# Far values of dilated attention: transposed products from scaled probabilities, added to the near values by identity products in PSUM

## What is computed

```python
for gi, (window, dilation) in enumerate(((128, 1), (512, 4), (2048, 16))):
    o, lse = dilated_window_group(q[:, :, gi], k_sh[:, :, gi], v_sh[:, :, gi], window, dilation)
    outs.append(o)
    lses.append(lse)
alpha = jax.nn.softmax(jnp.stack(lses, axis=0), axis=0)
o = jnp.sum(alpha[..., None] * jnp.stack(outs, axis=0), axis=0)
return o.reshape(bsz, seq, ATTN_OUT_WIDTH).astype(xn.dtype) @ w_o
```

## Time and profile before

| | |
|---|---|
| median of three runs | 1446.95 us (1443.18 to 1450.6) |
| the profiled execution's own time | 1444.98 us |
| its span, first to last instruction | 1443.3 us |
| TensorE's mean granted clock | 0.966 of full |
| busy: TensorE, VectorE, ScalarE, GpSimd | 92%, 72%, 60%, 25% of the span |
| the stretch that the change touches | about 1018 to 1100 us of the span |

### The profile page before, as it was taken

How to read it: one execution, slowest core, us unless ns; L and a number is a source line. 1 busy time by engine, 2 the same in 40 slices (tenths; PEclk the granted TensorE clock), 3 DMA queues, 4 the chain that set the end, 5 groups by cost and what they waited for, 6 DMA issues and landing times. The chain is left out here.

```text
span 1443.3 us, 28422 instructions
## 1 busy us (share of the span) xinstructions
PE 1332.6 (92%) x10965; PEld 1053.9 (73%) x10965; DVE 1034.2 (72%) x1381; ACT 860.8 (60%) x1316; POOL 366.8 (25%) x413
## 2 busy tenths in 40 slices
PE   6899997898899899999996999999998999999994
PEld 3577676777754788888884787878786788888873
DVE  6556845567653799999997436666445799899997
ACT  7735644465422588888883444445544588888882
POOL 2022445466700122233311100011110133233310
PEclk9999999999999999999998999999979999999998
DMA  6322300411571699999994432112131699999994
GB/s 195 117 88 88 117 15 3 108 33 40 151 287 69 224 376 386 385 382 387 385 362 160 142 89 79 59 59 88 60 117 73 239 392 386 388 385 376 385 345 182
DMA packets 159668, 295.90 MB, mean 205 GB/s; under 512 B 16989, under 2 KB 32477, under 8 KB 159568
## 3 DMA queue, kind: packets, MB, share of 16 engines
q1 hardware_dynamic: 150416, 278.21, 53.3%
q0 software_dynamic: 8928, 16.22, 3.0%
q10 hardware_dynamic: 224, 0.07, 0.0%
HBM read 280.35 MB, written 30.41 MB: 215 GB/s over the span
## 5 line engine op out<-in xcount | busy, mean ns | idle before, releaser
L1717 DVE TENSOR_TENSOR moe_wlo<-kept_raw,moe_whi 128x2048 fp32r<-128x2048 f32 x162 | 370.2, 2288 | 42.4 <-ACT moe_whi L1713 37.8
L1713 ACT ACTIVATE moe_whi<-kept_raw 128x2048 fp32r<-128x2048 f32 x192 | 365.3, 1919 | 38.7 <-DMA kept_raw<-in_moe_w_down_dram 16.5
L1724 PE MATMUL all_bank<-moe_whi,moe_xhi 128*128 128x512 f32 x512 | 203.8, 398 | 1.1 <-DVE moe_xlo L1773 1.1
L1726 PE MATMUL all_bank<-moe_whi,moe_xlo 128*128 128x512 f32 x512 | 199.6, 390 | 0.0
L1725 PE MATMUL all_bank<-moe_wlo,moe_xhi 128*128 128x512 f32 x512 | 199.6, 390 | 0.0
L1724 PEld LDWEIGHTS all_bank<-moe_whi,moe_xhi 128*128 128x128 f32 x512 | 96.1, 188 | 23.0 <-DVE moe_xlo L1773 1.5
L1726 PEld LDWEIGHTS all_bank<-moe_whi,moe_xlo 128*128 128x128 f32 x512 | 96.1, 188 | 20.5
L1725 PEld LDWEIGHTS all_bank<-moe_wlo,moe_xhi 128*128 128x128 f32 x512 | 96.2, 188 | 18.8
L1724 PE MATMUL all_bank<-moe_whi,moe_hhi 128*128 128x512 f32 x256 | 100.3, 392 | 3.0 <-issue 2.6
L2381 DVE SCALAR_TENSOR_TENSOR attn_wlo<-attn_xhat,all_par,attn_whi 128x512 fp32r<-128x512 f32 x64 | 43.8, 747 | 78.4 <-ACT attn_whi L2364 78.4
L1726 PE MATMUL all_bank<-moe_whi,moe_hlo 128*128 128x512 f32 x256 | 99.7, 389 | 0.0
(11 more groups left out here) (458 smaller groups left out, 2916.7 us busy)
## 6 DMA issues: line engine op xcount, KB each, us to landing
kept_raw<-in_moe_w_gate_dram SPq DMA_DIRECT2D x64, 1024.0 KB, 11.1
kept_raw<-in_moe_w_up_dram SPq DMA_DIRECT2D x64, 1024.0 KB, 12.3
kept_raw<-in_moe_w_down_dram SPq DMA_DIRECT2D x64, 1024.0 KB, 11.3
attn_xhat<-in_w_kv_dram SPq DMA_DIRECT2D x10, 1024.0 KB, 5.1
attn_xhat<-in_attn_w_q_dram SPq DMA_DIRECT2D x6, 1024.0 KB, 5.0
all_h<-in_rwkv_w_k_dram SPq DMA_DIRECT2D x4, 1024.0 KB, 9.0
all_h<-in_rwkv_w_v_dram SPq DMA_DIRECT2D x4, 1024.0 KB, 5.0
all_h<-in_rwkv_w_r_dram SPq DMA_DIRECT2D x4, 1024.0 KB, 5.0
```

Of the source, the lines that this page charges most:

```text
L1713: nc.scalar.activation(whi[slot % SPLITS][:, :], raw[slot % 6][:, :], ACT.Copy).then_inc(m["hi_ok"], 1)
L1717: nc.vector.tensor_tensor(wlo[slot % SPLITS][:, :], raw[slot % 6][:, :], whi[slot % SPLITS][:, :].bitcast(fp32), ALU.subtract).then_inc(m[ ...
L1724: nc.tensor.matmul(bank[b][:, :], hi[:, k0 + k, :], wh[:, k, :], start=begin and k == 0, stop=False)
L1726: ins = nc.tensor.matmul(bank[b][:, :], lo[:, k0 + k, :], wh[:, k, :], start=False, stop=end and k == 3)
```

## The change

Far values are now made with the values as weights (128x64) and the transposed probabilities moving (128 columns), so the result comes out transposed, head e of a pair on PSUM partitions 64e to 64e + 63. The accumulated near and middle values are added in the same bank by a product with the identity (a true product, no transpose). For this the probabilities must hold the factor 1/sum before they are transposed: VectorE's new `share(u)` multiplies them in place by the reciprocals (128x512), and the transposes of the far units wait for `shared` in place of `p_ok`. `far_output` and its two VectorE instructions per pair are gone, and so are `far_values` and `turn`; `far_and_turn(b)` stands for both, for b = 0 to 2 ahead of the last unit's transposes, for b = 3 in the place of `turn(3)`. ScalarE copies the last transposed probabilities, and splits the second half of `w_o`, later in its order.

```diff
--- before.py
+++ after.py
@@ -2314,8 +2314,8 @@
             s.sem, ["squared", "rms", "rstd_ok", "xhat_ok", "tr", "xh_ok", "xl_ok", "unit", "ev_a", "ev_d"])
         pool_order, mask_ok, res_mm, m2_ok, s_done, sm_ok, max_ok, p_ok, t_done, pt_ok, o_done, o_ev = map(
             s.sem, ["pool_order", "mask_ok", "res_mm", "m2_ok", "s_done", "sm_ok", "max_ok", "p_ok", "t_done", "pt_ok", "o_done", "o_ev"])
-        order, own_ok, stat_ok, d_ok, e_ok, faded, l_ok, inv_ok, scaled, far_done, weighed, merged, otr, out_done, h_ok = map(
-            s.sem, ["order", "own_ok", "stat_ok", "d_ok", "e_ok", "faded", "l_ok", "inv_ok", "scaled", "far_done", "weighed", "merged", "otr", "out_done", "h_ok"])
+        order, own_ok, stat_ok, d_ok, e_ok, faded, l_ok, inv_ok, scaled, shared, otr, out_done, h_ok = map(
+            s.sem, ["order", "own_ok", "stat_ok", "d_ok", "e_ok", "faded", "l_ok", "inv_ok", "scaled", "shared", "otr", "out_done", "h_ok"])
         piece_in = [s.sem(f"piece_in{i}") for i in range(2)]
         hi_ok, lo_ok, piece_used, oh_ok, ol_ok = map(s.sem, ["hi_ok", "lo_ok", "piece_used", "oh_ok", "ol_ok"])
         first_in, hi0_ok, lo0_ok, root_in = map(s.sem, ["first_in", "hi0_ok", "lo0_ok", "root_in"])
@@ -2425,9 +2425,6 @@
 
         def kept_or_pT(u):
             return kept[u - FAR_AT] if u >= FAR_AT else pT[u % 2]
-
-        def far_bank(hp):
-            return bank[(7, 4, 5, 6)[hp]]
 
         def out_bank(u):
             return bank[(7, 4, 5, 6, 0, 1, 2, 3)[u]]
@@ -2564,11 +2561,12 @@
                             ins.then_inc(ev_a, 1)
                         if beside(sl, kh, i) is not None:
                             attend(beside(sl, kh, i))
-            transposed(NU - 1)
-            split_hi(act, NP + 1)
             for b in range(4):
+                if b == 3:
+                    transposed(NU - 1)
                 act.wait_ge(otr, b + 1)
                 nc.scalar.activation(in_order(oh[:, b, :]), by_residue(bank[b][:, :]), ACT.Copy).then_inc(oh_ok, 1)
+            split_hi(act, NP + 1)
             nc.scalar.activation(ss[:, 0:1], g["eps"][:, 0:1], ACT.Sqrt).then_inc(root_in, 1)
             junk = lambda j, x: xhat[:, j, 512 * x:512 * x + 512]
             for j in range(J):
@@ -2618,6 +2616,12 @@
                 gi, hh, _ = units[u]
                 dve.wait_ge(l_ok, u - MID + 1)
                 V.reciprocal(fold(inv, hh), fold(lsum, hh)).then_inc(inv_ok, 1)
+
+            def share(u):
+                gi, hh, _ = units[u]
+                dve.wait_ge(inv_ok, u - FAR_AT + 1)
+                probs = pr[u % 2].rearrange("p (j t) -> p j t", j=J)
+                V.tensor_tensor(probs, probs, fold(inv, hh).rearrange("p (j x) -> p j x", x=1).to_broadcast([P, J, P]), ALU.mult).then_inc(shared, 1)
 
             def attend(u):
                 gi, hh, jp = units[u]
@@ -2647,18 +2651,7 @@
                     output(u - 2)
                 if u > FAR_AT:
                     inverse(u - 1)
-
-            def far_output(hp):
-                heads = slice(2 * hp, 2 * hp + 2)
-                dve.wait_ge(far_done, hp + 1)
-                dve.wait_ge(inv_ok, 2 * hp + 2)
-                by_head = lambda x: x.rearrange("p (h j v) -> p h j v", h=2, j=J)
-                rate = inv[:, :, heads].rearrange("p j (h x) -> p h j x", x=1).to_broadcast([P, 2, J, HD])
-                V.tensor_tensor(by_head(sm[hp % 2]), by_head(far_bank(hp)[:, :]), rate, ALU.mult).then_inc(weighed, 1)
-                total = oacc[:, :, P * hp:P * hp + P].rearrange("p j (h v) -> p h j v", h=2)
-                dve.wait_ge(weighed, hp + 1)
-                dve.wait_ge(scaled, 2 * hp + 2)
-                V.tensor_tensor(total, by_head(sm[hp % 2]), total, ALU.add).then_inc(merged, 1)
+                    share(u - 1)
 
             def rest(b):
                 dve.wait_ge(oh_ok, b + 1)
@@ -2687,14 +2680,10 @@
                             far_mask()
                         if v is not None:
                             attend(v)
+            rest(0)
             inverse(NU - 1)
-            dve.wait_ge(p_ok, NU)
-            far_output(0)
-            far_output(1)
-            rest(0)
-            far_output(2)
+            share(NU - 1)
             rest(1)
-            far_output(3)
             rest(2)
             rest(3)
             split_lo(dve, NP + 1)
@@ -2741,7 +2730,10 @@
                 ins.then_inc(s_done, 2)
 
             def transposes(u):
-                pe.wait_ge(p_ok, u + 1)
+                if u < FAR_AT:
+                    pe.wait_ge(p_ok, u + 1)
+                else:
+                    pe.wait_ge(shared, u - FAR_AT + 1)
                 if u >= 1:
                     pe.wait_ge(pt_ok, u)
                 for i in range(J):
@@ -2767,24 +2759,17 @@
                         ins = nc.tensor.matmul(bank[7][:, HD * j:HD * j + HD], pT[u % 2][:, P * j:P * j + P], v(j), start=True, stop=True)
                 ins.then_inc(o_done, 1)
 
-            def far_values(hp):
-                if hp == 0:
-                    pe.wait_ge(o_ev, FAR_AT)
+            def far_and_turn(b):
+                if b == 0:
                     evacuated(pe, NPROJ - 2)
                     evacuated(pe, NPROJ - 1)
-                elif hp < 3:
-                    pe.wait_ge(sm_ok, NU)
-                pe.wait_ge(pt_ok, FAR_AT + 2 * hp + 2)
-                for e in range(2):
-                    for j in range(J):
-                        hh, at = 2 * hp + e, J * HD * e + HD * j
-                        ins = nc.tensor.matmul(far_bank(hp)[:, at:at + HD], kept[hh][:, P * j:P * j + P], vv[2][:, j, HD * hh:HD * hh + HD], start=True, stop=True)
-                ins.then_inc(far_done, 1)
-
-            def turn(b):
-                pe.wait_ge(merged, b + 1)
+                pe.wait_ge(pt_ok, FAR_AT + 2 * b + 2)
+                pe.wait_ge(scaled, 2 * b + 2)
                 for j in range(J):
-                    ins = nc.tensor.transpose(bank[b][:, P * j:P * j + P], oacc[:, j, P * b:P * b + P], g["ident"][:, :])
+                    for e in range(2):
+                        hh = 2 * b + e
+                        nc.tensor.matmul(bank[b][HD * e:HD * e + HD, P * j:P * j + P], vv[2][:, j, HD * hh:HD * hh + HD], kept[hh][:, P * j:P * j + P], start=True, stop=False)
+                    ins = nc.tensor.matmul(bank[b][:, P * j:P * j + P], oacc[:, j, P * b:P * b + P], g["ident"][:, :], start=False, stop=True)
                 ins.then_inc(otr, 1)
 
             def product(u, kts):
@@ -2842,19 +2827,14 @@
                             pe.wait_ge(mask_ok, 1)
                             nc.tensor.matmul(bank[7][:, 0:P], residue[:, :], residue[:, :], start=True, stop=True).then_inc(res_mm, 1)
                         attend(v)
+            for b in range(3):
+                far_and_turn(b)
             transposes(NU - 1)
-            far_values(0)
-            far_values(1)
-            turn(0)
-            far_values(2)
-            turn(1)
-            far_values(3)
-            turn(2)
             pe.wait_ge(lo_ok, NP)
+            pe.wait_ge(o_ev, FAR_AT)
             for u in range(3):
-                pe.wait_ge(merged, u + 1)
                 product(u, range(0, 2))
-            turn(3)
+            far_and_turn(3)
             for u in range(3):
                 product(u, range(2, 3))
             product(3, range(0, 3))
```

## The result

The changed kernel takes 1472.13 us (median of four runs, 1467.32 to 1475.45), the kernel before, on the same chip, 1448.57 us. The ratio is 1.0172, with a 95% interval of 1.015 to 1.0194: about 24 us slower. The profiled execution took 1470.7 us, its span is 1469.0 us.

A forecast was written before the change was run, and what follows sets the result against it. TensorE was taken to set the attention stage's end. Waits +19.8, clock +3, tail -6 and +0.9 made +17.7 us on 1444.98, so 1462.7; 2 us more for the median gave 1464.7, rounded 1464.5, range 1455 to 1472 us.

The forecast's parts named there:

- signs named beforehand: Unit 26's transposes about 10.6 us after 25's, 7 us idle; 52 to 56 us to unit 30; output product after 11 to 16.
- Part 1, the waits: Far units 24 to 30: transposes wait for `share` in VectorE's order, +19.8 us, the largest at unit 26.
- don't hold each other: Far units: GpSimd's `scale` and VectorE's `share` read the same reciprocal without delaying one another; no cost.
- Part 2, the clock in the loop: New TensorE idle times bring half clock after unit 26 and from 29 or 30 on: +3 us, bounds 0 and 7.
- nearest to two returns such as the one at 873: Clock loss taken at 3 us, after an earlier fall at 869.8 that was back at 873.0 us.
- Part 3, the end: Three `far_and_turn` calls cover the last exponentials and share: -6 us; with `far_and_turn(3)` and the first output products, +0.9.
- their busy, wide products should bring it back on the way: Stage's end: the three `far_and_turn` calls restore full clock, taking 11.5 us; 13 instead of 19.9 with the transposes.
- half clock and all drains: Stage's end: the bound of the saving if the clock stays half and every tiling change drains, 0 us.
- The price of a call: One `far_and_turn` call takes 2.0 to 3.3 us, taken 2.5 at full clock and 5.0 at half.
- The thin cover: Moved `w_o` split: about 6.3 us, hidden by some 7 us of first-half output products; cover 0.7 us.
- The heavy case: Rival: half clock nearly throughout, and drains; clock +7, tail -1, `far_and_turn(3)` +2.5, total +28, 1475 us; chance 0.10.
- The other side: Rival: weight splits don't delay `share` of 26 and 29, waits cost 11.2; total -1, 1446 us, not slower; chance 0.04.

The follow-up runs named there:

- run 5: The changed kernel with dummy products in TensorE's idle times ahead of the transposes of units 25, 26, 27, 29 and 30, waits kept; 1458.88 us, ratio 1.006.
- run 1: The changed kernel without `share`, the multiplication by 1/sum; far units' transposes wait for the exponentials again; 1442.54 us, ratio 0.9949.
- run 2: The changed kernel with reciprocal and `share` of units 24 to 30 moved ahead in VectorE's order; 1453.21 us, ratio 1.0037.
- run 3: The changed kernel with reciprocal and `share` moved ahead in VectorE's order for units 26 and 29 alone; 1461.23 us, ratio 1.0078.
- run 6: The changed kernel with the identity product first in every second token tile of `far_and_turn`, so fewer column tiling changes; 1464.43 us, ratio 1.0134.
- run 9: run 2 with two `far_and_turn` calls ahead of unit 30's transposes, and unit 30's reciprocal and share behind the last copy of values; 1449.16 us, ratio 1.0013.
- run 7: The kernel before, with far values of the first three pairs of heads ahead of the last unit's transposes; 1441.12 us, ratio 0.9958.
- run 8: The kernel before, with far values, `far_output` and turns of first pairs ahead of the last transposes, and ScalarE's split during its wait; 1435.92 us, ratio 0.9924.
- run 4: The kernel before with `share` and its wait added, the old end kept except `far_output`'s own multiplication; 1474.35 us, ratio 1.0175.
- run 10: run 9 with the alternating product order of run 6 inside each `far_and_turn` call; 1447.79 us, ratio 0.9994.

## Why the prediction was off

The direction, the mechanism and its largest place were right. The time was not: 1464.5 us was forecast, and 1472.13 lies just above the range, whose upper end was 1472. On which side of that end the median fell is chance, since single runs differ by 8 us; that the size was wrong is not. In the two traces the last group of output products starts at 1102.5 us before and at 1129.5 us after: 27.0 us, 0.3 of it from earlier stages, against 17.7 forecast. The span grew by 25.7 us, the median of the runs by 23.6; the differences of 1 to 3 us between these three figures I can't assign, the runs of one kernel differ by more. Of the signs named beforehand, the place and length of the wait of unit 26 came (10.6 and 7.2 us); 58.1 us to unit 30 (52 to 56 named) and 17.9 us to the first output product (11 to 16) did not.

- **Part 1, the waits: right.** Forecast +19.8 us by unit 30, of which 18.2 from unit 24 to 30, that is 52.0 us. Run 5, where the clock fell only behind unit 24, measured 53.7 us: 11.3, 10.6, 9.8, 5.0, 10.5 and 6.5 us for units 25 to 30, where 9.8, 10.7, 9.8, 4.5, 10.5 and 6.7 were forecast. The 1.5 us too much for unit 25 are that half clock, and the 0.5 for unit 28 the slower `share` beside GpSimd, which the prediction took to be undisturbed ("don't hold each other"). Unit by unit the changed kernel gives +1.6, +4.1, +7.1, +3.7, +2.2, +3.4 and +3.9 us, where +1.6, +2.6, +7.2, +1.3, +1.3, +3.4 and +2.4 were forecast: units 24, 26 and 29 to 0.1, the others short by 1 to 2.5 us each, and these are the units with half clock in the slot ahead of them. That `share` makes these waits is shown by run 1, and that its place in VectorE's order makes half of their length, and with the clock most of the loss, by runs 2 and 3.
- **Part 2, the clock in the loop: mis-sized.** Taken at 3 us, with a bound of 7. The seven steps add up to 26.0 us, so it measured 6.2 as a difference; run 5, with the clock held from unit 25 on, shows 4.4 of it (58.1 less 53.7) and 1.5 more is the half clock ahead of its own unit 25. The step that failed is "nearest to two returns such as the one at 873". Falls were forecast behind unit 26 and from 29 or 30 on. The clock fell five times by unit 30, also behind unit 27 and already behind the 1.8 us for unit 24 (with 0.43 us just before it), and each time the scores and with them VectorE's part came later.
- **Part 3, the end: mis-sized, and this is the larger error.** The step that failed is "their busy, wide products should bring it back on the way" (13 instead of 19.9, taken -6). The fall ahead of the end was forecast; the return was not there. The clock stayed at half through all three calls and the end took 17.9: -2.0. The forecast's own end for "half clock and all drains" was 0. The gain of 1.2 us on the first output products did not come either, for the same reason. From the first output product to the last group of them, with the fourth call in between, go 26.4 instead of 23.6 us: +2.8 where +0.9 was forecast.
- **The price of a call** was 3.15 us at full and 5.4 us at half clock against 2.5 and 5.0, inside the range of 2.0 to 3.3. The change of column tiling, bounded at 0 to 0.16 us from the scores' row, costs 0.17 us (run 6), eight times a call: I had taken less than half of it (0.5 us a call, where eight are 1.4). The Trainium skill, TensorEngine Tiling (Array Packing), section Tiling Modes, Key Properties, says that changing the mode drains TensorE; run 6 agrees as far as each change has a price, and gives the number. That a drain is what takes the time, no run shows.
- **The thin cover** of the moved split held: TensorE has no idle time between the fourth call and the end of the output products.
- **The rivals.** The heavy case (half clock nearly throughout, and drains) was the nearest in every term that failed: it had +7, -1 and +2.5 us where +6.2, -2.0 and +2.8 were measured, and got 0.10. The other side's condition, splits not in the way, is made for just the two units in run 3, where 0.8% of loss is left, and for all units in run 2; its price of no loss is met only with the clock kept at the end as well (run 9). What the prediction lacked was to take its own row at its word: before the change, 16.7 us of unbroken fp32 work at the end had run at half clock to its end, and the return that it took as a model, at 873 us, came in dense products of 512 columns.

## What to carry to other kernels

Before an engine's input is made to depend on one more step of another engine, read where that step stands in the other's written order: 0.7 us of work cost 7 us behind a weight split. Price an idle time of TensorE by what runs after it as well as by itself: here the clock cost more than the net of the waits (1.1 against 0.6%), and a reordering of the old form that fills such a time (run 7 and run 8) gave more than the new form did in any version that keeps the factor 1/sum. The best version found is the old arithmetic with its independent products put ahead of the wait, 0.76% faster than the kernel before.

## What the runs showed of the hardware

- In the changed kernel the granted clock went from 1.00 to 0.50 behind idle times of 2.54 to 7.16 us, and behind 0.43 and 1.80 us close together; the last pair did so in all eight profiles of kernels with `share`. One of 2.54 us, ahead of unit 25, did not bring it down.
- Dense products of 512 columns saw it back within 2 to 5.5 us of their start. The column-tiled fp32 products with their eight changes a call did not in 17 us (three profiles), and with four changes a call it was back in 5 to 6 us (one profile).
- Filling those idle times with useless products made the changed kernel 0.9% (medians) to 1.1% (ratios) faster.
- A change between 64-column and 128-column products costs 0.17 us at full and 0.25 us at half clock (run 6).
- VectorE's multiplication of 128x512 with both inputs in SBUF took 0.69 to 0.70 us alone and 1.15 to 1.16 us when it started together with a GpSimd operation of 0.62 us. In seven profiles (the changed kernel, runs 2 to 5, 9 and 10) this holds for all 56 of them, 34 alone and 22 beside GpSimd. It was not tried by itself. The Trainium skill, SBUF — State Buffer, section Terms, says that the two engines share one port pair and that one is blocked while the other holds it; the 0.46 us more fit that, though no run shows the port itself.
